# A two-block transformer on one core: the first four tiles of each section made chunk by chunk, low weights kept over the raw ones, residual sums on VectorE

## The reference, cut to what matters

```python
for i in range(DEPTH):
    g = norm_g[i]
    h = h + 0.5 * rms_norm(swiglu(rms_norm(h, g[0]), ffn_wi[i, 0], ffn_wo[i, 0]), g[1])
    hn = rms_norm(h, g[2])
    y = dilated_mixer(hn, ...) if i == 0 else window_gqa_mixer(hn, ...)
    h = h + rms_norm(y, g[3])
    h = h + 0.5 * rms_norm(swiglu(rms_norm(h, g[4]), ffn_wi[i, 1], ffn_wo[i, 1]), g[5])
    e = p[i] @ ple_proj[i]
    gate = sigmoid(rms_norm(h, g[6]) @ ple_gate[i])
    h = h + rms_norm(e * gate, g[7])
```

## Time and profile before

| | |
|---|---|
| median of 3 runs | 3647.85 us (3646.64 to 3650.93) |
| the profiled execution's own time | 3644.68 us |
| its span, first to last instruction | 3642.9 us |
| TensorE busy, share of the span | 94% |
| VectorE, ScalarE, GpSimd busy | 50%, 34%, 12% |
| mean granted TensorE clock | 0.976 of full |

### The profile page before, as it was taken

One profiled execution on the slowest core, in us unless ns is written; L12 is line 12 of the kernel. 1 busy time (PEld: TensorE's weight loads), 2 busy tenths in 40 slices (PEclk: granted clock), 3 DMA queues, 4 the chain that ended last, 5 costly groups with the idle time before them and its releaser, 6 DMA issues.

```text
span 3642.9 us, 45046 instructions
## 1 busy us (share of the span) xinstructions
PE 3435.5 (94%) x16712; PEld 2670.3 (73%) x16712; DVE 1806.7 (50%) x2784; ACT 1227.2 (34%) x1853; POOL 424.9 (12%) x301
## 2 busy tenths in 40 slices
PE   8988999898899999999899799998899989899996
PEld 6666888676588867888677578785688856688774
DVE  5765333566543444443566544435544367544334
ACT  2354232324432333222333432223322235422223
POOL 0301000021100000000433200002100032200013
PEclk9999999999999999999999899999999999999998
DMA  4102222311122222223222123231222321122321
GB/s 160 62 30 69 95 96 94 115 64 36 47 98 92 98 69 87 98 98 104 87 72 70 35 92 97 93 104 64 69 98 98 104 66 47 58 97 93 98 92 46
DMA packets 81403, 299.97 MB, mean 82 GB/s; under 512 B 9040, under 2 KB 9040, under 8 KB 80640
## 3 DMA queue, kind: packets, MB, share of 16 engines
q1 hardware_dynamic: 78624, 284.20, 23.6%
q0 software_dynamic: 1568, 11.98, 0.9%
q10 hardware_dynamic: 1088, 2.10, 0.2%
HBM read 296.14 MB, written 2.10 MB: 82 GB/s over the span
## 4 chain that ended last, share of the span: by engine, by line
PE 83%; DVE 9%; ACT 4%; issue 2%; POOL 1%; DMA 1%; ACTq 0%; POOLq 0%; DVEq 0%
PE bank L717 20%; PE bank L718 20%; PE bank L719 20%; PE bank L953 5%; PE bank L955 4%; PE bank L954 4%; PE bank L772 2%; DVE wl L1644 1%; DVE prod L1712 1%; ACT wh L1261 1%; ACT sc L1397 1%; PE bank L1141 1%; PE bank L1153 1%; DVE x L1700 1%; DVE sc L1880 1%
## 5 line engine op out<-in xcount | busy, mean ns | idle before, releaser
L1644 DVE TENSOR_TENSOR wl<-raw,wh 128x1024 fp32r<-128x1024 f32 x538 | 690.6, 1284 | 601.4 <-ACT wh L1261 593.0
L717 PE MATMUL bank<-x,wh 128*128 128x512 f32 x2048 | 828.7, 405 | 51.6 <-DVE x L1700 24.3
L1261 ACT ACTIVATE wh<-raw 128x1024 fp32r<-128x1024 f32 x538 | 565.6, 1052 | 817.7 <-PE bank L719 539.3
L718 PE MATMUL bank<-x,wh 128*128 128x512 f32 x2048 | 803.0, 392 | 0.0
L719 PE MATMUL bank<-x,wl 128*128 128x512 f32 x2048 | 802.4, 392 | 0.0
L717 PEld LDWEIGHTS bank<-x,wh 128*128 128x128 f32 x2048 | 388.2, 190 | 158.1 <-issue 60.5
L717 PE MATMUL bank<-mid,wh 128*128 128x512 f32 x1216 | 481.1, 396 | 6.1 <-DVE wl L1644 6.1
L718 PE MATMUL bank<-mid,wh 128*128 128x512 f32 x1216 | 480.6, 395 | 0.0
L719 PE MATMUL bank<-mid,wl 128*128 128x512 f32 x1216 | 480.6, 395 | 0.0
L718 PEld LDWEIGHTS bank<-x,wh 128*128 128x128 f32 x2048 | 388.7, 190 | 91.2 <-issue 13.8
L719 PEld LDWEIGHTS bank<-x,wl 128*128 128x128 f32 x2048 | 388.1, 190 | 81.1
(11 more groups left out here) (271 smaller groups left out, 3239.5 us busy)
## 6 DMA issues: line engine op xcount, KB each, us to landing
raw<-stream SPq DMA_DIRECT2D x538, 512.0 KB, 3.3
sm<-small POOLq DMA_DIRECT2D x2, 2144.0 KB, 9.8
tb<-tab POOLq DMA_DIRECT2D x2, 1728.0 KB, 14.0
h<-x_t ACTq DMA_DIRECT2D x4, 512.0 KB, 7.1
out_t<-h SPq DMA_DIRECT2D x8, 256.0 KB, 2.0
tba<-tab_a POOLq DMA_DIRECT2D x1, 1152.0 KB, 7.8
pf<-p_t POOLq DMA_DIRECT2D x2, 512.0 KB, 3.8
tba<-tab_a POOLq DMA_DIRECT2D x1, 512.0 KB, 4.2
```

The lines of the kernel that those rows point to most:

```text
L717: pe.matmul(bk_[:, :], hi, src[:, kc, 0, :], start=start and j == 0, stop=False)
L718: pe.matmul(bk_[:, :], hi, src[:, kc, 1, :], start=False, stop=False)
L1261: act.activation(wh[n % 2][:, :], raw[n % 4][:, :], ACT.Copy).then_inc(hi_done, 1)
L1644: dve.tensor_tensor(wl[n % 2][:, :], raw[n % 4][:, :], wh[n % 2][:, :].bitcast(F32), ALU.subtract).then_inc(split_done, 1)
```

## The change

1. **First tiles together.** In an opening TensorE now makes chunk k of tiles 0, 1 and 2 when x chunk k is there, and chunk k-2 (k-4 in the embedding) of tile 3 behind them; behind a layer norm of block one two tiles are made so. This needs a bank for each (`banks_*`), so tiles go over banks 0, 1, 4, 5, and 6 or 7 where they are free, each with its own `bank_free`.
2. **Low weights over the raw ones.** `wl` n lies in the buffer `raw` n, and `wh` and `wl` have four buffers each. Splits run three units ahead, and a fourth is made at chunk 1 of an opening. SyncE loads unit n when TensorE has finished unit n-4. `AFTER_NORM` and `AFTER_EMBED` say how many splits follow each tile behind an opening.
3. **Residual sums on VectorE.** `h + prod` moves from GpSimd to VectorE (`add` in `residual`). The sum of squares moves from 8 `ones` matmuls to 7 additions on VectorE (`low_part`), and one `ones` matmul (`pre_sum`) behind tile 1.
4. **Embedding.** `ple_proj` makes 8 tiles over banks 6, 7, 5, 0, 1, 4, 6, 7 and `stat_sq` stands behind the first of them; they are copied to `emb` by ScalarE instead of VectorE.
5. The gate steps of the first mixers stand up to 7 pieces later (`PLACED`), and mixer B starts its scores at piece 38 instead of 30, with 2 pieces instead of 3 in every third step.

```diff
-TILES4 = dict(tile=4, used0=2, used1=2)
+TILES4 = dict(tile=4, used0=1, used1=1, used4=1, used5=1)
+def banks_first(i):
+    return (0, 1, 4)[i] if i < 3 else (i + 1) % 2
+def banks_up(i):
+    return (0, 1, 4, 5)[i % 4]
+def banks_gated(i):
+    return (0, 1, 4, 5, 6, 0, 1, 4)[i] if i < 8 else (5, 0, 1, 4)[i % 4]
+def banks_mixer(i):
+    return (0, 1, 4, 5, 7)[i] if i < 5 else (i + 1) % 2
+def banks_embed(i):
+    return (5, 0, 1, 4, 6, 5, 0, 1)[i]
+EMB_BANKS = ((6, 7, 5, 0), (1, 4, 6, 7))
+def together(width, lag=None):
+    order = []
+    for k in range(DC + (lag or 0)):
+        if k < DC:
+            order += [(t, k) for t in range(width)]
+        if lag is not None and k >= lag:
+            order.append((width, k - lag))
+    return order
+BY_TWO, BY_THREE, GATED = together(2), together(3, 2), together(3, 4)
+AFTER_NORM, AFTER_EMBED = (1, 0, 0, 1, 1, 2), (1, 1, 1, 0, 0, 1, 1, 2)
...
-        wh = [at(f"wh{i}", [P, UNIT], F32R) for i in range(2)]
-        wl = [at(f"wl{i}", [P, UNIT], F32R) for i in range(2)]
+        wl = [at(f"wl{i}", [P, UNIT], F32R, offset=place[0] + (i - 4) * UNIT * 4) for i in range(4)]
+        wh = [at(f"wh{i}", [P, UNIT], F32R) for i in range(4)]
...
             def load(k, wait=True):
                 if wait:
-                    sp.wait_ge(split_done, c.at("unit", back=3))
+                    sp.wait_ge(unit_done, c.at("unit", back=3))
...
             def square_sums():
                 acc_read()
+                c.wait(pre_done)
                 pool.memset(acc[:, :], 0.0).then_inc(acc_done, 1)
...
-            def add_parts():
-                for m in range(DC):
-                    c.wait(part_made)
-                    pool.tensor_tensor(h[:, m, :], h[:, m, :], prod[m % 2][:, :], ALU.add).then_inc(h_ready, 1)
...
+            def first_tiles(order, summed=True, before=None):
+                u, dst = c.n["unit"], {}
+                for t, kc in order:
+                    if t == 0:
+                        c.wait(x_ready)
+                    if kc == 0:
+                        if before is not None:
+                            before(t)
+                        dst[t] = free_tile()
+                        pe.wait_ge(split_done, u + t + 1)
+                    mm = piece(dst[t], u + t, kc * P, x, kc, kc == 0, kc == 7)
+                    if kc == 7:
+                        mm.then_inc(unit_done, 1)
+                        c.tick("unit")
+                        if t == 1 and summed:
+                            pre_sum()
...
+            def pre_sum():
+                c.tick("sq_made", DC)
+                c.wait(sq_used, DC)
+                pe.matmul(bank[3][:, :], ones[:, :], acc[:, :], start=True, stop=True).then_inc(pre_done, 1)
...
             def ffn2():
-                tiles_of(2 * FF2C, 4, x, ready=x_ready, also=square_sum)
+                c.start(banks_gated)
+                first_tiles(BY_THREE)
+                for k in range(4):
+                    tile(x)
...
-                read_all()
                 c.wait(p_ready, 2)
                 for n in range(2):
-                    pe.wait_ge(split_done, c.at("unit") + 1)
-                    if n == 1:
-                        c.wait(emb_read, 4)
-                    for j in range(4):
-                        unit(bank[4 + j], [j * 256, j * 256 + P], px, range(2), True, True, last=j == 3)
-                    if n == 0:
-                        stat_sq()
-                tiles_of(8, 2, x, ready=x_ready, also=square_sum)
-                c.wait(emb_read, 4)
+                    pe.wait_ge(split_done, c.n["unit"] + 1)
+                    for j, b in enumerate(EMB_BANKS[n]):
+                        pe.wait_ge(bank_free[b], c.n[f"used{b}"])
+                        if n == 1 and j >= 2:
+                            pe.wait_ge(emb_read, 8 * layer + j - 1)
...
+                        if n == j == 0:
+                            stat_sq()
+                c.start(banks_embed)
+                first_tiles(GATED, before=lambda t: pe.wait_ge(emb_read, 8 * layer + 3 + t))
...
-            def low_part(g, k, early=(4,)):
+            def low_part(g, k):
                 c.wait(x_hi)
                 dve.scalar_tensor_tensor(x[:, k, 1, :], h[:, k, :], vec[:, g + k:g + k + 1],
                                          x[:, k, 0, :].bitcast(F32), ALU.mult, ALU.subtract).then_inc(x_ready, 1)
-                if k in early:
-                    split_early()
+                if k:
+                    both = 2 if k == 1 else 1
+                    c.wait(sq_made, both)
+                    dve.tensor_tensor(acc[:, :], sq[0][:, :] if k == 1 else acc[:, :], sq[k % 2][:, :],
+                                      ALU.add).then_inc(sq_used, both)
+                    c.wait(sq_used, both)
+                if k == 1:
+                    split()
...
+                def add(k):
+                    c.wait(part_made)
+                    dve.tensor_tensor(h[:, k, :], h[:, k, :], prod[k % 2][:, :], ALU.add).then_inc(h_ready, 1)
+
                 part(0)
+                add(0)
                 part(1)
...
                 for k in range(DC):
+                    if k + 1 < DC:
+                        add(k + 1)
                     if k + 2 < DC:
                         part(k + 2)
```

More of the change, by code:

```diff
@@ L232, in plan_b @@
             yield "norm", s + 1
+        n = 3 if s % 3 else 2
         if len(b_blocks(s)) == 3:
@@ L705, in _, with piece @@
             c = Count(pe)
-            def unit(bk_, cols, src, chunks, start, stop, last=True, ready=None, also=None):
-                u = c.n.get("unit", 0) % 2
-                for j, (col, kc) in enumerate(zip(cols, chunks)):
+            def piece(dst, u, col, src, kc, start, stop):
+                hi, lo = wh[u % 4][:, col:col + P], wl[u % 4][:, col:col + P]
+                pe.matmul(dst, hi, src[:, kc, 0, :], start=start, stop=False)
+                pe.matmul(dst, hi, src[:, kc, 1, :], start=False, stop=False)
+                return pe.matmul(dst, lo, src[:, kc, 0, :], start=False, stop=stop)
@@ L711, in unit, with free_tile @@
+            def free_tile():
+                b = c.next_tile()
+                if c.n[f"used{b}"] > 1:
+                    pe.wait_ge(bank_free[b], c.at(f"used{b}", back=1))
+                return bank[b][:, :]
+            def unit(dst, src, chunks, start, stop, ready=None):
+                pe.wait_ge(split_done, c.at("unit") + 1)
+                for j, kc in enumerate(chunks):
                     if ready is not None:
                         c.wait(ready)
-                    if also is not None and j:
-                        also(j - 1)
@@ L736, in tiles_of @@
-            def tiles_of(n, per, src, spread=(range(8),), ready=None, also=None):
-                for k in range(per):
-                    tile(src, spread, *((ready, also) if k == 0 else ()))
-                with c.loop(n // per - 1, unit=per * len(spread), **(TILES4 if per == 4 else TILES2)):
-                    for k in range(per):
-                        tile(src, spread)
+                    mm = piece(dst, c.n.get("unit", 0), kc % 8 * P, src, kc, start and j == 0,
+                               stop and j == len(chunks) - 1)
@@ L1332, in rms_post, with tile_square @@
                 rstd(bank[2][:, :], 1)
-            def tile_square(n, last=False):
-                units(n, last)
+            def tile_square(n):
+                for k in range(n):
+                    c.wait(unit_done)
+                    if k < n - 1:
+                        split()
                 square_of(bank[c.next_tile()][:, :])
+                split()
             def square_of(src):
@@ L1481, in _ @@
                         up4(i + 1)
[L1482 to L1484 removed]
+                    with c.loop(2, split=8, unit_done=8, **TILES4):
+                        for k in range(4):
+                            for _ in range(2):
+                                c.wait(unit_done)
+                                split()
                             c.next_tile()
@@ L1940, in _ @@
             for layer in range(DEPTH):
-                for stage, k in plan_n():
+                c.start(banks_first)
+                for stage, k in plan_n(BY_TWO if layer else []):
                     if stage == "unit":
-                        units(1)
+                        c.wait(unit_done)
                         if k < N_PROJ:
-                            src = bank[c.n.get("tile", 0) % 2][:, :]
+                            src = bank[c.peek()][:, :]
                             if k in ROPED:
@@ L2086, in rest @@
                     else:
-                        units(1)
-                    free(dve.tensor_tensor(y[:, m, :], bank[c.n["tile"] % 2][:, :], y[:, m, :], ALU.add))
-                    if (m + 1) * n_units % 8 == 0 and m < DC - 1:
-                        split_early()
+                        c.wait(unit_done)
```

(3 more changed lines are left out.)

529 lines of the change are left out of this document (287 added, 242 removed).

## The result

The changed kernel takes 3548.76 us (median of 4 runs, 3544.13 to 3551.26), the kernel before 3649.03 us on the same chip (4 runs, 3646.64 to 3650.93). The ratio is 0.9724, 95% interval 0.9707 to 0.9741: faster by 100 us, where 106 were forecast. The profiled execution took 3549.39 us with a span of 3547.5.

The account below looks back on a forecast made before the run. The time was taken as TensorE's matmuls plus its losses between sections; gains at openings, embeddings, down tiles and the end, less 1 us, sum to 105.5 us: 3542 us for the median, forecast range 3526 to 3558 (60%).

Parts of the forecast that it names:

- The first matmul: In an opening behind a branch, TensorE starts 5.7 us behind the end of the statistics, against 6.54 before.
- VectorE's chunk: In an opening, VectorE's four operations (add, part, low part, sum) take 2.67 us a chunk.
- The rule of the Trainium skill that was weighed: Next VectorE operation waits for an empty pipe: chunk 2.84 us, 1 us more per opening, 8 in all; not used.
- TensorE sets the pace: In openings TensorE is full from its start; behind a branch the fourth tile ends 30.4 us behind the statistics.
- it isn't VectorE: Rival that VectorE sets the openings' pace: chunk 3.44 us, 3.7 us more in eight openings, 3572 us; 17%.
- The stops: TensorE waits for late units 4 and 5 behind openings: ffn 1.45 and 1.0 us, mixers 3.3 first, embedding 2.5 and 3.6.
- mixer A's second: In mixer A, unit 5 comes 3.4 us late because roped reads wait for GpSimd's operations of 2.29 us each.
- The end: At the kernel's end, eight parts and additions on VectorE alone take 11.2 us instead of 14.4: 3.2 gained.
- The clock's rival: TensorE's clock stays at half through eight openings, 19.4 us more each: 3697 us; 5% slower, 2% around break-even.
- The three openings of two tiles: Behind a layer norm, two tiles take 10.9 us plus 1.4 of half clock, from 16.0: 3.7 each, 11.1 gained.
- The moved steps: Moved gate steps and mixer B's steps with 2 pieces, priced by no row: 1 us lost.
- 33.2 and 5.2: Gains at the embeddings: 16.6 us twice for their openings, and 2.63 us waits of the first down tile before each.

Follow-up runs that it names:

- the short sums: The changed kernel with VectorE's additions of the squares of chunks 3 to 8 over 8 columns instead of 512: 3546.4 us, ratio 0.9726.
- the two profiles: The changed kernel profiled, and profiled again without an edit: medians 3548.76 us and 3546.8 us.

## Why the prediction was right, and where it wasn't

- **The first matmul** was put at 5.7 us behind the statistics: 5.66 to 5.76 in all five where x comes straight behind the statistics.
- **VectorE's chunk** was put at 2.67: 2.65. The rule of the Trainium skill that was weighed (VectorE: DVE Perf Modes, The DRAIN you can't avoid) would have made it 2.84. In the rows above three of the four operations start 0.61 to 0.67 us behind the one before, which is still shown for 0.69 to 0.74; only behind the sum, whose end the next one waits for, it is 0.71 after 0.68. The same section of the Trainium skill says that a next operation that isn't held starts earlier, and these rows agree with that.
- **TensorE sets the pace**: behind mixer A 30.3 us to the end of the fourth tile against 30.4, in the other four behind a branch without an embedding 30.3 to 31.2, behind the layer norm 29.2 against 29.4. That it isn't VectorE is shown by the short sums (no gain), that each matmul counts by the sums on TensorE (43 us for 56 products).
- **The stops**: in ffn 1.55 to 2.29 against 1.45, and then none to 0.81 against 1.0; mixer A 3.24 against 3.3 and then 1.78 against 3.4; mixer B 2.62 against 3.3, and its scores 2.22 and 0.61 against 4.2; embedding 2.41 against 2.5 and 4.16 against 3.6. The largest error is mixer A's second: its roped reads wait 1.27 and 1.38 us for GpSimd, not the 2.29 that an operation took in the earlier trace rows.
- **What the sum left out** is the clock behind a stop. The 24 matmuls behind mixer A's stop of 3.24 us take 7.1 us, and those behind mixer B's of 2.62 too, where 5.45 are due at full clock. In both mixers this 1.7 us makes up for stops that were put too high, so that 4.6 and 7.6 us against 4.3 and 7.2 are in part luck. In the kernel before, the 48 matmuls behind the embedding's 5.00 stop take 13.4 us, not the 10.9 of the sum: up to the fourth tile the embedding took 61.0 us and not 58.6, and takes 42.6 now against 42.0.
- **The end** was put at 3.2: from the last product of the statistics to the end it is 15.04 us instead of 18.24.
- **The clock's rival** is out for this change: 0.93 over the first 20 us of the opening. The Trainium skill's case (TensorE: Matmul & The Clock Gate, A second HAM failure mode: psum-queue depth-cycling) is that of short idle times between groups of matmuls while a kernel goes through its banks. The kernel before fits it: in the opening behind mixer A it goes between banks 0 and 3 with waits in between, and the granted clock is 0.50 from 2080 to 2086, 1.00 from 2087 to 2093, 0.52 to 2096 and 1.00 from 2097 on. The changed kernel goes through more banks without idling, and its clock rises once and stays up to the end of the opening. Tiles one after the other idle 5.8 us in an opening in one bank, and the clock stays at half. So as far as these runs show it is the idle times and not the banks.
- **The three openings of two tiles** were forecast at 3.7 each: 48 matmuls in 12.3 us instead of 16.0. They take 12.4 to 13.0 in the two profiles; before, it was 16.0 in the first of them and 15.2 in the third (in the second, a step of the mixer stands in between). That is 2.1 to 3.6 each. The rest of the shortfall is in the second section, which has layer 1's mixers woven in: 299.2 us before, 297.7 and 300.3 in the two profiles. Over the three it is 7.9 in one profile and 4.1 in the other, for 11.1. This is the term that was too large.
- **The moved steps** were put at -1, which the table has at the start, though the term was also for mixer B's. It can't be told: the first stretch scatters by 11 us from run to run.

Where the sum was right, the credit inside it was not. Read alone, "side by side" and "sums off TensorE" look like 45 and 43 us of the 100; undone together they are 24, and with the additions 41. The other 60 came with the buffers, the banks and the copies of the embedding, 44 of it where the embeddings are, in the terms that the prediction summed as 33.2 and 5.2 there. Which of these makes up the 60 wasn't tried one by one; 26 of it are the stops of the earlier trace rows that are gone.

## What to carry to other kernels

Two chains run through an opening: VectorE makes the chunks, TensorE works them off, and the longer one counts. Moving the sums of squares takes 7 us off TensorE's chain and puts 4 on VectorE's. That gains only if the tiles side by side have made TensorE's the longer one; with one tile at a time it costs 22 us. Tiles side by side in turn gain at most 0.7 us in an opening behind a branch, less than the stops they bring, while TensorE still has the sums. So the two are worth something only as a pair, and undoing one alone mis-states both. Cut both traces at the first matmul of each section: block two's sections repeat within 0.9 us between the two profiles, where the whole time moves by 7. Once an opening is dense, its stop comes from what is freed last (here the first tile's buffer, its load, copy and low part), and an order of splits that gains in one section can lose in another.

## What the runs showed of the hardware

- One after the other, TensorE is idle for 5.8 us in the first 16 of an opening, and its granted clock is at half for 18 us (0.55 over 20). Where it has hardly any gaps the clock is back at full after 3 to 4 us (0.93 and 0.89 over the first 20 us). While TensorE waits for VectorE anyway, the half clock costs next to nothing.
- A stop can be followed by a stretch at half clock, which costs 1.7 us, and its length alone doesn't tell. Behind mixer A a stop of 2.29 us is followed by one and a stop of 1.58 isn't, as the next rows show (20 us in the changed kernel, then with the short sums: 0.91 and 1.00, 70 matmuls and 76). But the embedding's stop of 2.41 us is followed by half clock in one profile and not in another, with the same program there, and behind mixer B's of 2.62 the clock is 0.72 over the next 6 us in the changed kernel and 1.00 with the additions on GpSimd. The prediction counted stops without this.

```profile
2083.45:2103.45 20.00, 17.71 (x70) 13.87 (x69) 9.73 (x13) 9.10 (x12) 0.52 (x1) 0.91 0.43 155
```

```profile
2075.73:2095.73 20.00, 17.68 (x76) 13.66 (x75) 10.57 (x14) 10.34 (x13) 0.52 (x1) 1.00 0.40 138
```

- A program's sparse stretch costs different times in different executions: 304.6 to 315.7 us for the same 1877 matmuls, with a clock from 0.98 to 0.94.
- A VectorE operation over 128x512 float32 takes 0.68 to 0.75 us, and 1.75 to 1.78 while GpSimd adds two tiles of the same size in SBUF.
- A 512 KB load that takes 3.3 us as a median took 6.7 when four of them and another transfer of 512 KB were under way in 14 us.
